# Held-back sums, a norm taken apart at a stage's end, and a residual loaded by token halves in a hybrid decoder layer

## The reference

```python
proj = h @ w_in
gq, gk, gv, g_lr, g_gate, hq, hf, hi, h_gate = jnp.split(proj, IN_OFFSETS, axis=-1)
...
forget = lb + (1.0 - lb) * jax.nn.sigmoid(hf.astype(f32))
o_hgrn = chunk_gated_linear_attention(
    split_heads(jax.nn.silu(hq.astype(f32)), HGRN_HEADS),
    split_heads(1.0 - forget, HGRN_HEADS),
    split_heads(hi.astype(f32), HGRN_HEADS),
    split_heads(jnp.log(forget), HGRN_HEADS), CHUNK)
o_hgrn = merge_heads(rms_norm(o_hgrn, hgrn_norm_g)).astype(h.dtype) * jax.nn.silu(h_gate)
return jnp.concatenate([o_gla, o_hgrn], axis=-1) @ w_out
```

## Time and profile before

| what | value |
|---|---|
| median of three executions | 1164.97 us |
| profiled execution | 1166.44 us |
| its span | 1164.7 us |
| TensorE busy | 1137.4 us, 98% of the span |
| VectorE busy | 876.3 us, 75% |
| ScalarE busy | 612.9 us, 53% |
| GpSimd busy | 499.4 us, 43% |
| chain that ended last, TensorE's share | 89% |
| mean granted TensorE clock | 0.993 |

### The profile page before, as it was taken

How to read it: one execution, slowest core, us unless ns; L and a number is a source line. 1 busy time by engine, 2 the same in 40 slices (tenths; PEclk the granted TensorE clock), 3 DMA queues, 4 the chain that set the end, 5 groups by cost and what they waited for, 6 DMA issues and landing times.

```text
span 1164.7 us, 15675 instructions
## 1 busy us (share of the span) xinstructions
PE 1137.4 (98%) x5555; PEld 939.3 (81%) x5555; DVE 876.3 (75%) x1048; ACT 612.9 (53%) x933; POOL 499.4 (43%) x318
## 2 busy tenths in 40 slices
PE   7999999899999999999999999999999999999996
PEld 6788788787878787888888888888888888788885
DVE  6898888877777677477976765677795884966776
ACT  7763564756566566345654555455664433424424
POOL 1021111534243344427534353344466675666741
PEclk9999999999999999999999999999999999999999
DMA  9777353044353549421455344544624637447203
GB/s 359 259 235 271 128 175 97 1 127 129 93 177 98 154 123 295 143 93 73 137 170 181 136 155 135 181 144 157 194 64 159 223 91 264 147 132 279 72 1 145
DMA packets 160549, 180.44 MB, mean 155 GB/s; under 512 B 7508, under 2 KB 119256, under 8 KB 157784
## 3 DMA queue, kind: packets, MB, share of 16 engines
q1 hardware_dynamic: 160472, 179.44, 46.4%
HBM read 138.51 MB, written 40.89 MB: 154 GB/s over the span
## 4 chain that ended last, share of the span: by engine, by line
PE 89%; DVE 4%; DMA 2%; ACT 2%; issue 1%; SPq 1%; POOL 1%; DVEq 0%; ACTq 0%
PE unit_bank L1742 16%; PE unit_bank L2156 9%; PE unit_bank L2158 9%; PE unit_bank L2157 9%; PE small_bank L2156 9%; PE small_bank L2158 9%; PE small_bank L2157 9%; PE unit_bank L2003 3%; PE small_bank L1742 3%; PE unit_bank L2005 3%; PE unit_bank L2004 3%; PE small_bank L1879 2%; DVE ada_acc L2257 1%; PE small_bank L1781 1%; DMA ada_slot<-in_w_ada_dram 1%
## 5 line engine op out<-in xcount | busy, mean ns | idle before, releaser
L997 POOL TENSOR_TENSOR wr_lo<-quarter,wr_hi 128x512 fp32r<-128x512 f32 x122 | 197.6, 1632 | 174.4 <-ACT wr_hi L1530 174.3
L2156 PE MATMUL unit_bank<-op_hi,wr_hi 128*128 128x512 f32 x452 | 176.5, 390 | 1.1 <-issue 1.1
L2158 PE MATMUL unit_bank<-op_hi,wr_lo 128*128 128x512 f32 x452 | 175.9, 389 | 0.0
L2157 PE MATMUL unit_bank<-op_lo,wr_hi 128*128 128x512 f32 x452 | 175.9, 389 | 0.0
L2156 PE MATMUL small_bank<-op_hi,wr_hi 128*128 128x512 f32 x448 | 174.5, 390 | 0.0
L2158 PE MATMUL small_bank<-op_hi,wr_lo 128*128 128x512 f32 x448 | 174.3, 389 | 0.0
L2157 PE MATMUL small_bank<-op_lo,wr_hi 128*128 128x512 f32 x448 | 174.3, 389 | 0.0
L1530 ACT ACTIVATE wr_hi<-wr_full 128x512 fp32r<-128x512 f32 x90 | 56.8, 631 | 173.3 <-DVE wr_full L2903 173.3
L2903 DVE TENSOR_TENSOR wr_full<-quarter,quarter 128x512 f32<-128x512 f32 x90 | 88.9, 989 | 56.3 <-PE small_bank L2158 23.0
L1530 ACT ACTIVATE wr_hi<-quarter 128x512 fp32r<-128x512 f32 x136 | 83.0, 626 | 90.5 <-PE unit_bank L2158 48.4
L1742 PE MATMUL unit_bank<-a_hi,w_hi 128*128 128x512 f32 x304 | 121.2, 399 | 0.8 <-DVE w_lo L2401 0.8
(11 more groups left out here) (366 smaller groups left out, 2397.2 us busy)
## 6 DMA issues: line engine op xcount, KB each, us to landing
quarter<-in_w_mlp_dram SPq DMA_DIRECT2D x128, 256.0 KB, 4.1
hidden_scratch<-hid SPq DMA_DIRECT2D x98, 256.0 KB, 2.4
ada_slot<-in_w_ada_dram SPq DMA_DIRECT2D x48, 512.0 KB, 6.1
op_full<-hidden_scratch SPq DMA_DIRECT2D x21, 1024.0 KB, 4.8
pair_quarter<-in_w_in_dram SPq DMA_DIRECT2D x32, 256.0 KB, 3.7
piece_x<-t_scratch SPq DMA_DIRECT2D x16, 512.0 KB, 4.1
piece_y<-t_scratch SPq DMA_DIRECT2D x32, 256.0 KB, 3.3
raw<-in_w_out_dram SPq DMA_DIRECT2D x16, 512.0 KB, 4.5
```

What stands on the lines that cost most here:

```text
L997: pool.tensor_tensor(wr_lo[slot][:, :, :], split_source(n), wr_hi[slot][:, :, :].bitcast(F32), ALU.subtract).then_inc(wr_lo_pool, 1)
L2156: pe.matmul(dst, wh, ah, start=opens, stop=False, skip_group_check=True)
L2157: pe.matmul(dst, wh, al, start=False, stop=False, skip_group_check=True)
L2158: mm = pe.matmul(dst, wl, ah, start=False, stop=k == KH - 1, skip_group_check=True)
```

## The change

It has seven parts.

- The pieces with an even number come as two DMAs of 256 KB in place of one of 512 KB, on the same queue.
- x is loaded back by token half. The order on SyncE around it is new.
- ScalarE makes `sq_hi` ahead of the copy of the output to `mixed`, in every stage.
- At the end of a paired stage ScalarE's Ln for half 1 stands behind the next pair's P7 high part, and the Exp behind two readings of results and the P2 high part.
- TensorE's `attend(8)` stands behind the late pair's P4 and no longer ahead of it.
- In H0 VectorE makes S2 of the first pair ahead of the decay copy and `q_cum`; `add_parts` waits for the low part of P2.
- At the end of a paired stage VectorE makes `sq_lo` of half 1 behind two joins, and the norm's scaling at the very end.

```diff
--- before.py
+++ after.py
@@ -711,11 +711,8 @@
                     sp.wait_ge(normed, before("ss", 3))
                 if p == 5 and j == 0:
                     sp.wait_ge(mixed_out, MIXED_OUT_0 + 16)
-                if j % 2:
-                    for i in range(2):
-                        sp.dma_start(piece_y[i][:, :].bitcast(F32), t3_dram[:, j, i, :]).then_inc(piece_y_loaded, 16)
-                else:
-                    sp.dma_start(piece_x[120 if p < 5 else 96][:, :, :].bitcast(F32), t3_dram[:, j]).then_inc(piece_x_loaded, 16)
+                for i, part in enumerate(piece_place(p, j)):
+                    sp.dma_start(part.bitcast(F32), t3_dram[:, j, i, :]).then_inc(piece_y_loaded if j % 2 else piece_x_loaded, 16)
 
             def load_pair_quarter(p, i):
 
@@ -759,12 +756,11 @@
                 sp.wait_ge(seventh_done, SEVENTH_0 + 4 * PAIRS - 1)
                 sp.dma_start(mixed[:, 0, :], mixed_dram).then_inc(mixed_back, 16)
 
-            def load_x_back(i):
+            def load_x_back(i, half):
 
                 sp.wait_ge(six_done, six_of(PAIRS - 1, P4 if i else P5))
-                for half in range(2):
-                    part = slice(half * HALF, (half + 1) * HALF)
-                    sp.dma_start(xT[:, 4 * i:4 * i + 4, part], x_dram[:, 4 * i:4 * i + 4, part]).then_inc(x_back[i][half], 16)
+                part = slice(half * HALF, (half + 1) * HALF)
+                sp.dma_start(xT[:, 4 * i:4 * i + 4, part], x_dram[:, 4 * i:4 * i + 4, part]).then_inc(x_back[i][half], 16)
 
             def load_out(v):
 
@@ -832,10 +828,12 @@
             load_out(0)
             load_mixed_back()
             load_out(1)
-            for i in range(2):
-                load_x_back(i)
-            for v in range(2, 4):
-                load_out(v)
+            load_x_back(0, 0)
+            load_out(2)
+            load_x_back(1, 0)
+            load_out(3)
+            load_x_back(0, 1)
+            load_x_back(1, 1)
             sp.wait_ge(normed, before("ss", 7))
             sp.wait_ge(seventh_done, SEVENTH_0 + 4 * PAIRS)
             for i in range(4):
@@ -1336,9 +1334,9 @@
                     src = bank_of("o", half)
                     act.wait_ge(normed, before("o", gi) + half)
                     act.activation(stat[:, 0, :], src, ACT.Square).then_inc(o_squared, 1)
-                    act.activation(tok(mixed[:, gi + 1], half), src, ACT.Copy).then_inc(read["o"], 1)
                     act.wait_ge(o_squared, before("o", gi) + half + 1)
                     act.activation(sq_hi[:, 0, :], stat[:, 0, :], ACT.Copy).then_inc(sq_hi_ready, 1)
+                    act.activation(tok(mixed[:, gi + 1], half), src, ACT.Copy).then_inc(read["o"], 1)
 
                 def norm_log(half):
 
@@ -1430,12 +1428,12 @@
                 pair_high(late + 1, P1)
                 act.wait_ge(filled["o"], before("o", gi + 1))
                 value_of(1, late, "22")
+                pair_high(late + 1, P7)
                 norm_log(1)
-                norm_exp(1)
-                pair_high(late + 1, P7)
-                pair_high(late + 1, P2)
                 value_of(0, late, "21")
                 tanh_of(t0, 1, late, "12")
+                pair_high(late + 1, P2)
+                norm_exp(1)
 
             def gates(gi):
 
@@ -2017,7 +2015,7 @@
                 if j % 2:
                     pe.wait_ge(piece_y_loaded, PIECE_Y_0 + 64 * p + 32 * (j // 2 + 1))
                 else:
-                    pe.wait_ge(piece_x_loaded, PIECE_X_0 + 32 * p + 16 * (j // 2 + 1))
+                    pe.wait_ge(piece_x_loaded, PIECE_X_0 + 64 * p + 32 * (j // 2 + 1))
                 wh, wl = pw_hi[place][:, j, :], pw_lo[place][:, j, :]
                 hi, lo = piece_place(p, j)
                 pe.matmul(dst, wh, hi, start=j == 0, stop=False, skip_group_check=True)
@@ -2066,8 +2064,8 @@
                 seventh_piece(late, 2)
                 pair_product(late, P5)
                 seventh_piece(late, 3)
+                pair_product(late, P4)
                 attend(8)
-                pair_product(late, P4)
                 pair_product(late, P3)
                 open_banks.clear()
                 open_banks.update(used)
@@ -2578,6 +2576,8 @@
                     weight_sum_of(0, "S3")
                     low_second()
                 read_out(6)
+                if own == "H":
+                    weight_sum_of(0, "S2")
                 if prev:
                     dve.wait_ge(read["up"], before("chunks", gi) + (30 if prev == "P" else 15))
                 dve.wait_ge(e_cum, gi + 1)
@@ -2589,7 +2589,7 @@
                 if name == "P1":
                     low_third()
                 if own == "H":
-                    weight_sum_of(0, "S2")
+                    dve.wait_ge(pair_lo, PAIR_LO_0 + split_of(0, P2))
                     add_parts(xs[2], 1, 0, 7)
                     subtract(xs[2], xs[2], xs[3], 8)
                 read_out(7)
@@ -2762,18 +2762,18 @@
                 dve.wait_ge(q_cum_ready, gi + 1)
                 dve.scalar_tensor_tensor(q_rel[:, :], q_rel[:, :], 0.5, t0[:, :], ALU.mult, ALU.mult).then_inc(q_rel_ready, 1)
                 weight_sum_of(late, "S4")
-                low_squares(1)
                 join(late, "u")
                 join(late, "22")
+                low_squares(1)
                 silu_of(t0, 0, late, "11", made + 3)
                 gate_half(tok(t0, 0), h, 0, ("11", late + 1), False)
                 weight_sum_of(late + 1, "S3")
+                join(late, "21")
                 weight_sum_of(late + 1, "S2")
-                join(late, "21")
-                norms(1)
                 join(late, "12")
                 silu_of(t0, 1, late, "12", made + 4)
                 gate_half(tok(t0, 1), h, 1, ("12", late + 1))
+                norms(1)
 
             def low_mixed(half, tiles=range(1, KT, 2)):
                 for k in tiles:
```

## The result

The changed kernel took 1171.82 us (median of five executions, 1170.72 to 1172.76); the kernel before, run beside it, 1165.19 us. The ratio is 1.0049, with a 95% interval from 1.0035 to 1.0063: 4.1 to 7.3 us slower. The profiled execution took 1172.76 us, its span 1171.0 us.

The account below looks back on a forecast made before the run. TensorE, busy 1137.4 of 1164.7 us, bounds the kernel, so only its waits and clock count. First pair 1.0, head ends 2.1, output projection 1.4 and clock 1.7 sum to +6.2 us: forecast 1171.2 us, range 1162 to 1177.

Parts of the forecast that it names:

- head ends: Ends of the late pairs, three heads: S3 falls behind GpSimd's low part, TensorE ends 0.7 us later each, +2.1 us.
- first pair: First pair: waits for low parts go, but later `q_cum` delays `k_nat`; TensorE idles 4.9 us; +1.0 us.
- the clock falls as it did before: First pair: the idle time for `k_nat` brings the low clock, as the earlier waits did; part of +1.0 us.
- Pieces in halves: Split piece loads: eight pieces' extra issues cost SyncE some 0.4 us each, hidden; 0, bounds -0.3 and +0.3 us.
- S3 keeping its place: Head ends: S3 stays ahead of GpSimd, -0.9 us; part of the no-change rival, about 1165 us, chance 0.19.
- Output projection: Output projection: third block's 0.8 us wait goes, but x loads behind the fourth's wait delay the fifth block; +1.4 us.
- The clock: Head ends and output projection: new idle times could lower TensorE's clock at four places; one fall counted, +1.7 us.
- Half 0: Half 0 of paired stages: `sq_hi` comes about 0.5 us earlier, but GpSimd still holds `sq_lo`; 0 us.
- S3 ahead of GpSimd at all three head ends: Head ends: named as a sign that the forecast is wrong; S3 was expected behind GpSimd's P1.
- The sign at the seventh product's first piece: Head ends: TensorE was to wait over 1 us at the seventh piece, behind SiLU.
- the wait for `k_nat`: First pair: a TensorE wait of about 4.9 us for ScalarE's `k_nat` was to appear ahead of the updates.
- the late fifth block: Output projection: the fifth weight block was to land after 461 us, in place of 459.5.

Follow-up runs that it names:

- order at the output alone: Kernel before with only SyncE's order at the output projection changed (x by token halves, third and fourth weight blocks earlier); 1.0027, +3.1 us.
- paired stages: Kernel before with only the paired-stage edits (`sq_hi` first, new ends of ScalarE, VectorE and TensorE), pieces not split; 1.0035, +4.1 us.
- with early `sq_lo`: Kernel before with the paired-stage edits, but `sq_lo` of half 1 kept ahead of the joins and the last Exp behind the `v_nat` copies; 0.9969, -3.6 us.
- both that helped: Paired-stage edits with `sq_lo` kept ahead of the joins, plus all x loads ahead of the fourth weight block; against the kernel before 0.9976, median 1162.16 us.
- the two other output orders: Kernel before with one x load ahead of the third weight block, three between it and the fourth (0.9991); or two ahead, two between (0.9997).
- pieces alone: Kernel before with only the even-numbered pieces loaded as two DMAs each; 1.0001.
- paired stages with split pieces: Kernel before with the paired-stage edits and the pieces as two DMAs each; 0.9991.
- end of H0 alone: Kernel before with only S2 ahead of the decay copy and `q_cum`, and `add_parts` behind P2's low part; 1.0030, +3.5 us.

## Why the prediction came out right, point by point

The forecast was +6.2 us, and the medians differ by 6.6. The sum is closer than its terms, and that is luck: the term of the head ends was too large, and that of the first pair too small.

**First pair: right in mechanism, too small.** Forecast was an idle time of 4.9 us for `k_nat` and +1.0; the trace has 4.64 us and +1.63, and the kernel with this part alone has +3.5 us. The step that was mis-sized is "the clock falls as it did before". The mean granted clock over 225 to 249 us shows it, in the profiles of all kernels that have this place as it was, and of the two with the change there:

| kernel | granted clock |
|---|---|
| before; order at the output alone | 0.86, 0.86 |
| paired stages; with early `sq_lo`; both that helped; the two other output orders; pieces alone | 0.93 each |
| paired stages with split pieces | 1.00 |
| the change; end of H0 alone | 0.86, 0.86 |

What this is worth shows in the lengths. With the place as it was, P1 to the first y piece takes 16.74 us in the two profiles with 0.86, 15.35 to 15.59 in the six with 0.93, and 15.29 in the one with 1.00. The profile that I read had more of the low clock than most profiles of the same code, and I took it for the rule. Against the six, the end of H0 alone (18.21 us) loses 2.6 to 2.9 us and the change (18.37) 2.8 to 3.0, nearer to the 3.5 measured. That is worked out from one profile for each kernel and not shown by runs made for it. The mean granted clock, which was taken of every execution, points the same way: 0.9922 over the eight of the end of H0 alone, 0.9948 over the 22 of the kernel before on the same chip. Over 1166 us the difference is about 3 us of full speed. That is the most it can have cost, since part of the low clock can fall into idle time, and it doesn't say at which place.

**Head ends: the mechanism stood, one edit's price did not.** Forecast was +0.7 each with S3 behind GpSimd. That is what the kernel without the split pieces does, to within 0.05 us at the seventh piece. With them S3 wins, by 0.04 us at the closest, and a head end costs 0.2 us. The three cost 0.7 us in all, where 2.1 were forecast. The step that failed is "Pieces in halves [...] 0": alone they make no difference that the time shows (1.0001), but they moved a landing by 0.2 us and more, and that decided between S3 and GpSimd. The forecast had this as a rival, S3 keeping its place, and gave it 0.9 us of gain; TensorE did gain 0.3 us up to the seventh piece at each head, but then lost 0.5 us around the copies of `v_nat`, 0.31 of it a plain wait, which I had not followed. By the Trainium skill ("SBUF — State Buffer", section "SBUF: two separate sides") whichever of the two starts first holds the port for its whole instruction. The traces agree at the margin: a lead of 0.04 us kept S3 at 0.69 us, and a lag of 0.19 us made it 1.79.

**Output projection: right.** Forecast +1.4; the trace has +1.47, that of the order alone +1.58 over the stage. The fifth block landed late, 3.3 us later behind `out` than before, for the reason given.

**The clock: right in number in the profile, perhaps too small over the executions.** I counted one fall of 1.7 us at a head end or here. It came behind the 2.42 us wait for the fifth block: that block to the MLP's start is 1.77 us longer. At the head ends, with 0.7 to 1.0 us of idle time, it stayed at full speed; without the split, behind 1.5 us, it fell once in three. But the mean clock over the executions is 0.9926 for the output order alone (eight) and 0.9913 for the paired stages alone (six), against the same 0.9948. That is about 2.5 and 4 us at most, of the 3.1 and 4.1 us that they lost; where in the kernel it falls is not shown. The five executions of the changed kernel have 0.9916.

**The rest.** Half 0 gained nothing, as forecast: the stretches with it differ by 0.06 us at most. The parts add up: 0.30% for H0, 0.27% for the output order and -0.09% for the paired stages with the split pieces make 0.48%, each with about 0.1% either way, and the whole change measured 0.49%.

**What would have shown me wrong** was named: S3 ahead of GpSimd at all three head ends. It was. By that sentence the head term was wrong, and the total stood because the first pair's was too small by about as much. The sign at the seventh product's first piece, a wait of over 1 us, did not come either (0.69 to 0.95 us); the wait for `k_nat` and the late fifth block did.

## What to carry to other kernels

A wait that is taken off the engine that sets the end is won only as far as the next operand for that engine is early: here the low parts were exchanged for `k_nat`, and that for a load that waits for a norm. Where two instructions of VectorE and GpSimd come up within 0.2 us of each other, any edit that moves a landing can decide between them, so an edit that seems to cost nothing still has to be priced at such places. In a queue that is worked in order, look at what is queued when an issue waits: a load moved ahead of others is paid for by those that then stand behind the wait.

## What the runs showed that I had not expected

The same code at the first pair was granted a mean clock of 0.86, 0.93 or 1.00 over 24 us in different profiles, and P1 to the first y piece took 16.74, about 15.5 and 15.29 us with them. One profile is a poor basis for the cost of the clock at a place with idle times of 0.8 and 1.9 us; the mean clock of many executions is a better one. Early in the kernel, in a stretch that no edit touched, traces differed by up to 2.7 us (the start of P1 at 224.7 to 227.4).
